# Latent attention: the first scores of a group between its value tiles, low parts by head pair, the last value tiles copied by VectorE

## The reference, cut to what matters

```
def queries(cq, length):
    q = (rms_norm(cq, q_norm_w) @ wq_b).reshape(bsz, length, C_HEADS, C_NOPE + C_ROPE)
    return q[..., :C_NOPE], q[..., C_NOPE:]

def keys_values(ckv, k_rope, length):
    kv = (rms_norm(ckv, kv_norm_w) @ wkv_b).reshape(bsz, length, C_HEADS, C_NOPE + C_V)
    k_rope_h = jnp.broadcast_to(k_rope[:, :, None, :], (bsz, length, C_HEADS, C_ROPE))
    return jnp.concatenate([kv[..., :C_NOPE], k_rope_h], axis=-1), kv[..., C_NOPE:]

def mla_core(q, k, v):
    s = jnp.einsum('bqhd,bkhd->bhqk', q, k).astype(F32) * ((C_NOPE + C_ROPE) ** -0.5)
    p = jax.nn.softmax(s, axis=-1)
    return jnp.einsum('bhqk,bkhd->bqhd', p.astype(v.dtype), v)
```

## Time and profile before

| what | value |
|---|---|
| median of 3 runs | 1672.2 us (1671.59 to 1674.89) |
| the profiled execution, its own time | 1673.72 us |
| its span in the trace | 1671.9 us |
| TensorE busy | 1546.6 us (93%) |
| VectorE busy | 908.2 us (54%) |
| ScalarE busy | 522.1 us (31%) |
| mean granted clock of TensorE | 0.987 of full speed |
| first layers and attention (to about 1093 us) | TensorE nearly always busy |
| experts (from about 1093 us) | DMA engines nearly always busy |

### The profile page before, as it was taken

One profiled execution on the slowest core, in us unless ns is written; L12 is line 12 of the kernel. 1 busy time (PEld: TensorE's weight loads), 2 busy tenths in 40 slices (PEclk: granted clock), 3 DMA queues, 4 the chain that ended last, 5 costly groups with the idle time before them and its releaser, 6 DMA issues.

```text
span 1671.9 us, 22739 instructions
## 1 busy us (share of the span) xinstructions
PE 1546.6 (93%) x8476; PEld 1065.4 (64%) x8476; DVE 908.2 (54%) x1571; ACT 522.1 (31%) x836; POOL 155.5 (9%) x203
## 2 busy tenths in 40 slices
PE   6999999799999989999999999899999998998985
PEld 2788888578788768787788777785343332332441
DVE  2876527687468556566787887975212121121124
ACT  3422221488143254444432476231000000000011
POOL 2000010034011000001302210210000000000003
PEclk9999999799999999999999999999999999999998
DMA  9334353102223310223444112359999999999995
GB/s 383 117 145 156 115 197 130 58 14 96 92 109 115 141 52 9 110 80 152 172 152 155 48 52 87 126 206 368 416 423 422 423 423 423 422 423 423 421 380 212
DMA packets 57619, 353.07 MB, mean 211 GB/s; under 512 B 7376, under 2 KB 7632, under 8 KB 20544
## 3 DMA queue, kind: packets, MB, share of 16 engines
q1 hardware_dynamic: 43200, 307.41, 45.9%
q0 software_dynamic: 9248, 35.63, 5.8%
q10 hardware_dynamic: 5088, 8.92, 1.4%
HBM read 332.53 MB, written 23.59 MB: 213 GB/s over the span
## 4 chain that ended last, share of the span: by engine, by line
PE 66%; DMA 14%; DVE 9%; ACT 4%; SPq 3%; issue 3%; POOL 1%; ACTq 0%; DVEq 0%; POOLq 0%
PE ps L2274 11%; PE ps L2276 11%; PE ps L2275 11%; DMA early<-in_experts 10%; PE ps L2835 8%; PE ps L2315 4%; PE ps L2855 4%; PE ps L2793 3%; SPq L708 3%; PE ps L2498 3%; PE ps L2522 2%; DMA early<-in_ada 2%; PE ps L2515 1%; PE ps L2226 1%; PE ps L2420 1%
## 5 line engine op out<-in xcount | busy, mean ns | idle before, releaser
L2274 PE MATMUL ps<-whi,xth 128*128 128x512 f32 (+1 forms) x768 | 300.1, 391 | 3.8 <-DVE xtl L1736 1.8
L2276 PE MATMUL ps<-whi,xtl 128*128 128x512 f32 (+1 forms) x768 | 296.5, 386 | 0.0
L2275 PE MATMUL ps<-wlo,xth 128*128 128x512 f32 (+1 forms) x768 | 296.1, 386 | 0.0
L2835 PE MATMUL ps<-early,xe_t 128*64 128x512 f32 x904 | 207.2, 597 | 31.1 <-DMA early<-in_experts 25.4
L2835 PEld LDWEIGHTS ps<-early,xe_t 128*64 128x64 f32 x904 | 60.9, 136 | 171.5 <-issue 105.1
L2274 PEld LDWEIGHTS ps<-whi,xth 128*128 128x128 f32 x768 | 144.8, 188 | 34.8 <-DVE xtl L1736 3.5
L2276 PEld LDWEIGHTS ps<-whi,xtl 128*128 128x128 f32 x768 | 144.6, 188 | 29.4
L2275 PEld LDWEIGHTS ps<-wlo,xth 128*128 128x128 f32 x768 | 144.9, 189 | 27.7
L2108 DVE TENSOR_TENSOR hid<-hid,ps 128x256 f32<-128x256 f32 x33 | 13.9, 421 | 251.1 <-ACT hid L1288 251.1
L1344 DVE TENSOR_TENSOR wlo<-raw,whi 128x2048 fp32r<-128x2048 f32 (+3 forms) x52 | 103.2, 1984 | 62.1 <-ACT whi L914 61.3
L1288 ACT ACTIVATE hid<-ps 128x256 f32<-128x256 f32 x33 | 12.7, 384 | 391.5 <-PE ps L2835 391.5
(11 more groups left out here) (463 smaller groups left out, 2686.3 us busy)
## 6 DMA issues: line engine op xcount, KB each, us to landing
early<-in_experts SPq DMA_DIRECT2D x128, 1024.0 KB, 26.5
raw<-in_experts SPq DMA_DIRECT2D x51, 1024.0 KB, 24.5
raw<-in_ada SPq DMA_DIRECT2D x40, 1024.0 KB, 6.5
ring<-in_experts SPq DMA_DIRECT2D x15, 1024.0 KB, 27.8
raw<-in_even SPq DMA_DIRECT2D x14, 1024.0 KB, 5.4
raw<-in_second SPq DMA_DIRECT2D x10, 1024.0 KB, 5.0
early<-in_ada SPq DMA_DIRECT2D x8, 1024.0 KB, 18.5
pair_dram<-tmp ACTq DMA_DIRECT2D x60, 128.0 KB, 6.8
```

What stands on the lines that cost most here:

```text
L2274: nc.tensor.matmul(v, a[0], b[0], start=first, stop=False)
L2275: nc.tensor.matmul(v, a[0], b[1], start=False, stop=False)
L2276: return nc.tensor.matmul(v, a[1], b[0], start=False, stop=last)
L2835: mm = nc.tensor.matmul(ps[SLOT * t:SLOT * t + SLOT, 4 + s, :], xe_t[:, 2 * i + k, SLOT * s:SLOT * s + SLOT], w[:, D * k + 512 * t:D * k + ...
```

## The change

It does four things.

1. The value tiles of a group now lie in slots 2 and 3 by turns (v0 in 2, v1 in 3, v2 in 2, ...), and the scores of the first pair (still slots 0 and 1) stand in TensorE's order between the value tiles 1 and 2. The wait for the value tiles is put behind the scores of the second pair (`kept`), ahead of the first `O`.
2. The waits before the scores are split by head pair: heads 0 and 1 need only their own `q`, `kv` tiles and the first `qr_l`. DVE's order follows: the two `k_l` of a pair, then `qr_l` of that pair.
3. `ada(2, 2)` in group 1 moves from behind the value tiles to ahead of them on TensorE (its slot is now 0), and on DVE from behind the last `qr_l` to behind the first.
4. Of the six value tiles ACT copies the first four; the last two are copied by DVE, behind its two maxima.

```
 def attention_jobs(plan, stage, units, between=None):
-    for u in units[0:2]:
-        plan.job("S", stage, u, slot=u % 2)
...
-        for m in tiles:
-            plan.pieces[-1]["last"] = plan.job("v", g, m)
         if g:
             ada(2, [2])
+        for m in tiles:
+            if m == 2:
+                for u in range(16 * g, 16 * g + 2):
+                    plan.job("S", "odd", u, slot=u % 2)
+            plan.pieces[-1]["last"] = plan.job("v", g, m, slot=2 + m % 2)
...
-                for m in range(NT):
+                for m in range(4):
                     v = filled(act, "v", g, m)
...
-                for f in range(4):
-                    low(("kv", g, f), k_h[:, f, :], k_l[:, f, :], 8 * g + f + 5, TOK, 1.0)
                 for j in range(2):
+                    for f in (2 * j, 2 * j + 1):
+                        low(("kv", g, f), k_h[:, f, :], k_l[:, f, :], 8 * g + f + 5, TOK, 1.0)
                     dve.wait_ge(s_qr_hi, 2 * g + j + 1)
                     own.free(nc.vector.tensor_tensor(qr_l[:, j, :], tmp[:, j, 0:SEQ], qr_h[:, j, :].bitcast(F32),
                                                      ALU.subtract), s_qr_lo)
-                if g:
-                    ada(2, 2)
+                    if g and not j:
+                        ada(2, 2)
                 maximum("odd", 16 * g, s_nbo)
                 maximum("odd", 16 * g + 1, s_nbo)
+                for m in range(4, NT):
+                    v = filled(dve, "v", g, m)
+                    own.free(nc.vector.tensor_copy(v_o[:, m, :], v[:, 0:512]), ev("v", g, m))
...
-                score(units[0])
                 for u in units[::2]:
                     for w in (u, u + 1):
...
                     if u + 2 in units:
                         score(u + 2)
+                    if u == units[0]:
+                        kept()
...
             def odd_scores(u):
                 m, h = u % 16 // 4, u % 4
+                if u % 16 < 4:
+                    for f in (h, h + 1):
+                        evacuated(pe, "q", u // 16, f)
+                        evacuated(pe, "kv", u // 16, f)
+                    pe.wait_ge(s_qr_lo, 2 * (u // 16) + h // 2 + 1)
...
+                def values_kept():
+                    for m in tiles:
+                        evacuated(pe, "v", g, m)
+
                 for m in tiles:
+                    if m == 2:
+                        pe.wait_ge(s_kr_lo, 1)
+                        odd_scores(16 * g)
                     v = begin("v", g, m)
...
-                for f in range(4):
-                    evacuated(pe, "q", g, f)
-                    evacuated(pe, "kv", g, f)
-                for m in tiles:
-                    evacuated(pe, "v", g, m)
-                pe.wait_ge(s_kr_lo, 1)
-                pe.wait_ge(s_qr_lo, 2 * g + 2)
```

More of the change, by code:

```diff
@@ L2484, in _, with attend_pairs @@
             banks = ((0, 512), (512, TOK))
-            def attend_pairs(stage, units, score, pbuf, pts, v_of, n, between=None):
-                score(units[0])
+            def attend_pairs(stage, units, score, pbuf, pts, v_of, n, kept):
                 for u in units[::2]:
@@ L2500, in attend_pairs @@
                         end(mm, "O", stage, w)
-                    if between and u == between[0]:
-                        between[1]()
             passes = ((0, 0), (0, 1), (1, 0))
@@ L2546, in _ @@
                     end(mm, "kv", g, f)
+                if g:
+                    ada(2, 2)
+                def values_kept():
+                    for m in tiles:
+                        evacuated(pe, "v", g, m)
                 for m in tiles:
+                    if m == 2:
+                        pe.wait_ge(s_kr_lo, 1)
+                        odd_scores(16 * g)
                     v = begin("v", g, m)
@@ L2551, in _ @@
                         "v", g, m)
-                if g:
-                    ada(2, 2)
-                for f in range(4):
-                    evacuated(pe, "q", g, f)
-                    evacuated(pe, "kv", g, f)
-                for m in tiles:
-                    evacuated(pe, "v", g, m)
-                pe.wait_ge(s_kr_lo, 1)
-                pe.wait_ge(s_qr_lo, 2 * g + 2)
                 attend_pairs("odd", range(16 * g, 16 * g + 16), odd_scores, po[g], [pto[g][:, 0, :], pto[g][:, 1, :]],
-                             lambda u, a: v_o[:, a, P * (u % 4):P * (u % 4) + P], P)
+                             lambda u, a: v_o[:, a, P * (u % 4):P * (u % 4) + P], P, values_kept)
             def gate(layer, first, n=0):
```

## The result

The changed kernel is slower: 1678.9 us (median of 12 runs, 1671.8 to 1685.6) against 1673.4 (median of 12, 1671.0 to 1675.7), a ratio of 1.0033 with a 95% interval of 1.0019 to 1.0048. The forecast was 1673.3, in a range of 1670.5 to 1676.0; against its base of 1672.2 that is 1.1 us slower, and 5.4 were measured. The profiled execution took 1685.6 us, with a span of 1683.8 us and a granted clock of 0.973.

What follows compares the result with a forecast made beforehand. TensorE was taken as the bound (66% of the chain). Group 0 +1.0 and group 1 -0.65 gave +0.35 us; 1673.3 us is the middle of 1674.1 and 1672.55, depending on slow stretches in the median's runs; range 1670.5 to 1676.0.

Steps and rivals of the forecast that it cites:

- Group 0, step 1, the slot wait: Group 0: value tile 0 waits for slot 2, freed by the fourth `k_l`; TensorE idle 4.3 us instead of 1.13.
- Steps 2 to 4, the schedule and the table load: Group 0: earlier scores, value tiles under the softmax, but an uncovered 1.28 us table load before the exponential; loses 1.0 us.
- The load's drain: Rival, ACT in group 0: a drain behind the table load delays the exponential 1.4 us more, 1674.7 us; chance 0.03.
- Group 1, the schedule: Group 1: new hole of 1.4 us before value tile 0, hole before transposes 2.14 to about 0.1; gains 0.65 us.
- the prediction's own sign: Group starts: the prediction called itself wrong if DVE's 0.69 us copies held up the transposes.
- The clock, group 1: Group 1 loses its long hole, so no slow stretch there, where the profiled execution had one of 1.55 us.
- The clock, group 0 and the sum: Group 0: one slow stretch of 1.55 us behind the 4.3 us hole; both groups' schedule without the clock sums to +0.35 us.
- The two cancel: Group 0's new slow stretch and group 1's lost one, 1.55 us each, offset each other against the profiled execution.
- The slower rival: Group 0, 595 to 612 us: the long hole throttles TensorE twice, 2 x 1.55 us, giving 1676.4 us; chance 0.13.
- The base and the range: Whole kernel: base median 1672.2 us from three runs spanning 3.3 us; range 1670.5 to 1676.0 us.

Runs made afterwards that it cites:

- The control: The kernel before, unaltered, run again beside the kernel before: 1675.7 us against 1674.7, ratio 0.9997.
- the first comparison: The changed kernel's first measurement against the kernel before: 1678.9 us against 1673.4, ratio 1.0033.
- the second set: The changed kernel run once more, unaltered, against the kernel before: 1676.1 us against 1675.0, ratio 1.0005.
- the filled kernel: The changed kernel with idle TensorE time in both group starts filled by products nobody reads: 1672.4 us, ratio 0.9990 to the kernel before.

## Why the prediction was wrong

- *Group 0, step 1, the slot wait:* right. 4.31 us of idle time against 4.3.
- *Steps 2 to 4, the schedule and the table load:* right. At full clock 19.57 us, 0.86 over before, against 1.0; the hole ahead of the transposes 1.34 against 1.4. The load's drain, which the Trainium skill gives ("ScalarE: Activation LUTs", What ACT_TABLE_LOAD costs: about 1380 ns more), isn't in the trace: the exponential starts 1.30 us after the load's start. That rival falls.
- *Group 1, the schedule:* the hole of 1.4 us is 1.25, the hole ahead of the transposes 0.25 instead of 0.1, and VectorE's copy is what ends it, by the prediction's own sign a small miss (it had the copy nearly as late, not later). This group never ran at full clock with the change's order, so the gain of 0.65 us was not measured by itself.
- *The clock, group 1:* the step that failed. "Group 1 loses its long hole, so I take none there": all three profiles have a long stretch there, and a price of 20.8 - 18.5 = 2.3 us if the forecast schedule (20.72 - 1.55 - 0.65 = 18.5) is taken for full clock. The control agrees with that: group 1 of before took 19.11 us at full clock, and 19.11 - 0.65 = 18.5. I had counted `ada(2, 2)` as work that fills a hole. The rows of the five starts with this order (0.80 us idle, 1.7 us of one-column products, 1.25 us idle) say otherwise: half clock set in during the products in two of them (at 692.9 in the first comparison, at 686.2 in the second set), so ahead of the second hole, and at the products' end or in the second hole in the other three.
- *The clock, group 0 and the sum:* in group 0 I priced the stretch by the one of before, 1.55 us; it measured 21.18 - 19.57 = 1.6 to 22.25 - 19.57 = 2.7. "The two cancel" left +0.35 against the profiled execution; 3.2 us were lost locally. Put together, both starts would take 19.57 + 18.5 = 38.1 us at full clock and took 42.6 in the mean of the three profiles: 4.5 us of clock, where one stretch of 1.55 was forecast, while before has about 1.5. The reading behind the price was loose too: the trace has a longer idle stretch than the 4.47 us of the earlier trace rows, the 13.41 us ahead of the first product.
- *The slower rival* had the right mechanism and a wrong place: two stretches, but in groups 0 and 1, not both in group 0. It gave 1676.4, that is 4.2 us over its base of 1672.2; over all sets the change costs 2.4, in the first comparison 5.4. That 1676.4 lies near the mean of 1677.9 is partly luck, since the base is 1675.5 there.
- *The base and the range:* three runs within 3.3 us of each other were taken for the scatter. Over 112 runs the kernel before goes from 1669.4 to 1685.0 us. Its two traces differ already ahead of the change: the first `k_l` starts at 591.15 and 594.72, with a granted clock of 0.83 and 0.77 in 320 to 360 us. How much of the whole scatter is of this kind isn't shown. The upper bound of 1676.0 was too near for that alone, and some 3 of the 5.4 us of the first comparison didn't come again.

Not tried: the one-column products without the hole of 0.80 us ahead of them, and the two holes without the products. Known is that a hole of 3.11 us without them brings half clock too, that with the second hole filled to 0.28 us it still came, and that with `ada(2, 2)` ahead of the key tiles it didn't.

## What to carry to other kernels

When a job is moved to another PSUM slot, look whose evacuation it now waits for: a slot can turn a wait of 1 us into one of 4 without any line of the change saying so. Price a hole on TensorE at its length plus the half clock that comes behind it (here 1.6 to 2.7 us behind 3.7 to 4.3 us), don't count on tiny products to break up a hole, and if it can't be closed, try to fill it: group 0 lost its half clock by that, group 1 only part of it. For effects of a few us compare the stretch itself in the profile, since here one program's time scatters with a standard deviation of 3.3 us, in part ahead of the edit.

## What was not expected of the hardware

All thirteen group starts with a hole of 3.1 to 4.3 us (eight), or with two smaller ones around the one-column products (five), had half clock in them; so had group 1 of the filled kernel, whose holes are 0.80 and 0.28 us around the one-column products and the filler. Work that nobody reads made group 0 1.6 to 2.7 us shorter. The other seven changed starts, whose holes are under 1.8 us with no one-column products between them, had none; of the five unchanged starts, with a hole of 2.1 us ahead of the transposes, three had one.
